# Self-attention with values as weights: two heads side by side in 64-column tiles

## The reference

```python
def causal_block_attention(q, k, v, scale, log_decay=None):
    ...
    def one_block(args):
        i, qi = args[0], args[1]
        s = jnp.einsum('bhqd,bhkd->bhqk', qi, k, preferred_element_type=jnp.float32) * scale
        if log_decay is not None:
            s = s + args[2][..., :, None] - log_decay.astype(jnp.float32)[:, :, None, :]
        ...
        s = jnp.where(mask, s, jnp.finfo(jnp.float32).min)
        p = jax.nn.softmax(s, axis=-1)
        return jnp.einsum('bhqk,bhkd->bhqd', p.astype(v.dtype), v)
```

## Time and profile before

| | us |
|---|---|
| runs, median of 3 | 3243.78 |
| profiled execution, its own time | 3245.3 |
| span of the profile | 3243.0 |
| self-attention stage, from the first scores to the last values | 392.5 to 755.5 |
| TensorE busy, whole span | 2861.4 (88%) |
| VectorE busy, whole span | 1193.4 (37%) |
| ScalarE busy, whole span | 612.3 (19%) |
| mean granted TensorE clock, share of full speed | 0.944 |

### The profile page before, as it was taken

One profiled execution on the slowest core, in us unless ns is written; L12 is line 12 of the kernel. 1 busy time (PEld: TensorE's weight loads), 2 busy tenths in 40 slices (PEclk: granted clock), 3 DMA queues, 4 the chain that ended last, 5 costly groups with the idle time before them and its releaser, 6 DMA issues.

```text
span 3243.0 us, 53552 instructions
## 1 busy us (share of the span) xinstructions
PE 2861.4 (88%) x19249; PEld 2455.6 (76%) x19250; DVE 1193.4 (37%) x3107; ACT 612.3 (19%) x1355; POOL 196.7 (6%) x257
## 2 busy tenths in 40 slices
PE   7999899999999996879988889899989998898980
PEld 5444477775477765879988889889989998898980
DVE  1111166663212226324322234323335443343446
ACT  0333233332011111111110111111111111111211
POOL 0000000001000001001000000000001000000100
PEclk9999899999999997989999999899999998999995
DMA  6111311122100006557554567456557875676737
GB/s 246 43 55 45 106 35 44 45 88 80 71 33 0 0 0 247 205 191 257 199 191 157 199 239 292 176 185 226 216 219 283 295 280 195 227 273 228 288 121 265
DMA packets 91043, 530.87 MB, mean 164 GB/s; under 512 B 20528, under 2 KB 42224, under 8 KB 65264
## 3 DMA queue, kind: packets, MB, share of 16 engines
q1 hardware_dynamic: 70992, 490.27, 41.8%
q0 software_dynamic: 18720, 33.60, 2.9%
q10 hardware_dynamic: 1152, 4.19, 0.3%
HBM read 510.14 MB, written 52.46 MB: 173 GB/s over the span
## 4 chain that ended last, share of the span: by engine, by line
PE 83%; issue 8%; DVE 4%; DMA 2%; ACT 2%; DVEq 1%; ACTq 1%; POOL 0%; POOLq 0%; SPq 0%
PE bank L989 48%; PE wide L989 22%; PE bank L982 5%; PE wide L1092 4%; PE bank L1109 3%; DMA ye<-d_y 1%; PE bank L1273 1%; DVE acc L1840 1%; ACT prob L819 1%; ACT st_q L799 1%; DVE mx L1497 1%; DVEq L1799 0%; PE wide L1095 0%; DVE biased L1502 0%; DVE act_t L1805 0%
## 5 line engine op out<-in xcount | busy, mean ns | idle before, releaser
L989 PE MATMUL bank<-xe_t,slot 128*128 128x128 f32 (+2 forms) x8192 | 1089.9, 296 | 187.2 <-issue 187.2
L989 PEld LDWEIGHTS bank<-xe_t,slot 128*128 128x128 f32 x8192 | 1077.2, 197 | 194.8 <-issue 194.3
L989 PE MATMUL wide<-act_t,slot 128*128 128x128 f32 (+2 forms) x4096 | 535.1, 290 | 8.4 <-DVE act_t L1805 7.6
L989 PEld LDWEIGHTS wide<-act_t,slot 128*128 128x128 f32 x4096 | 522.9, 191 | 13.3 <-DVE act_t L1805 13.2
L1793 DVE TENSOR_SCALAR glu<-bank,b_gu 128x256 f32<-128x256 f32 x256 | 123.8, 484 | 1011.3 <-PE bank L989 999.4
L931 ACT ACTIVATE sig<-glu 128x256 f32<-128x256 f32 x256 | 106.7, 417 | 1070.3 <-DVE glu L1793 1016.4
L989 PE MATMUL bank<-w_in,xt 128*128 128x512 f32 (+1 forms) x512 | 216.5, 579 | 3.8 <-DVEq L1426 3.8
L938 ACT ACTIVATE y_t<-wide,b_dn 128x256 f32<-128x256 f32 x256 | 107.3, 470 | 461.1 <-PE wide L989 461.1
L989 PEld LDWEIGHTS bank<-w_in,xt 128*128 128x128 f32 x512 | 96.7, 191 | 111.1 <-issue 110.4
L689 POOL DMA_INDIRECT xg<-d_xn,gidx x66 | 68.2, 1034 | 1727.8 <-DVEq L1708 1717.7
L1805 DVE TENSOR_TENSOR act_t<-lin,sig 128x256 f32<-128x256 f32 x256 | 109.3, 427 | 39.9 <-issue 5.0
(11 more groups left out here) (242 smaller groups left out, 2488.0 us busy)
## 6 DMA issues: line engine op xcount, KB each, us to landing
slot<-in_w_gu SPq DMA_DIRECT2D x128, 2048.0 KB, 7.8
slot<-in_w_dn SPq DMA_DIRECT2D x64, 2048.0 KB, 7.8
ye<-d_y SPq DMA_DIRECT2D x8, 2048.0 KB, 10.4
w_in<-in_w_in SPq DMA_DIRECT2D x1, 6144.0 KB, 30.9
w_mem_k<-in_w_mem_kv SPq DMA_DIRECT2D x1, 4096.0 KB, 15.8
w_mem_v<-in_w_mem_kv SPq DMA_DIRECT2D x1, 4096.0 KB, 25.6
x_sb<-in_x SPq DMA_DIRECT2D x8, 512.0 KB, 3.6
cneg<-d_cneg SPq DMA_DIRECT2D x8, 512.0 KB, 4.9
```

The lines of the kernel that those rows point to most:

```text
L989: m = pe.matmul(dst, l, r_, start=(k == 0), stop=(k == n - 1))
```

## The change

The steps of a pass are put in another order: each block row is now done for MLA head h and forget head h in turn, so `B_STEPS` runs (MLA 7, forget 7, MLA 0, forget 0, MLA 6, ...). In `values` the operands are swapped: 64 columns of values are held and 128 columns of transposed probabilities are streamed. The MLA head's product goes to PSUM partitions 0 to 63 and the forget head's to 64 to 127, in two column tiles of TensorE, block by block in turn. The result is transposed (values by queries), so VectorE copies it to SBUF (`turned`), TensorE transposes it back (`turn_back`), and `attended` scales both halves into `o_sb`. The values of a head are first copied by GpSimd from `v_mla` and `v_fox` into `v_head`. Transposed probabilities have four buffers, queries, keys and biases two of each (`side`), `biased` has one. The load of `w_xq` is moved behind the stage's barrier, among the loads of the next stage. Some semaphores are merged so that their number suffices.

```diff
-        B_STEPS = [(0, i) for i in long_short] + [(1, i) for i in long_short]
-        B_FIRST, B_LAST = (0, NT), (NT - 1, 2 * NT - 1)
+        B_STEPS = [(y, i) for i in long_short for y in range(2)]
+        B_FIRST, B_LAST = (0, 1), (2 * NT - 2, 2 * NT - 1)
@@ SyncE
-            load(w_xq[:, :, :], rows(a["w_xq"][0]), ld["w_xq"])
             barrier(sp, 3)
-            load(w_xo[:, :, :], rows(a["w_xo"][0]), ld["w_xo"])
-            load(w_r[:, :, :], rows(a["w_router"][0]), ld["w_r"])
-            with sp.Fori(0, NT) as i:
+            x_rows_again(0)
+            load(w_xq[:, :, :], rows(a["w_xq"][0]), ld["x_weights"])
+            x_rows_again(1)
+            load(w_xo[:, :, :], rows(a["w_xo"][0]), ld["x_weights"])
+            load(w_r[:, :, :], rows(a["w_router"][0]), ld["x_weights"])
+            with sp.Fori(2, NT) as i:
+                x_rows_again(i)
@@ GpSimd
+            def head_values(h, u, b):
+                po.wait_ge(b_v[b].free, u + 1)
+                for y, v in enumerate((v_mla, v_fox)):
+                    c = po.tensor_copy(v_head[b][y][:, :, :], v[:, :, bass.ds(h * S.DV, S.DV)])
+                c.then_inc(b_v[b].full, 1)
@@ TensorE
-                for j in range(i + 1):
-                    m = pe.matmul(pp[b][:, 0:S.DV], prob_t[b][:, j, :], v[:, j, bass.ds(h * S.DV, S.DV)],
-                                  start=j == 0, stop=j == i)
-                return m.then_inc(b_po[b].full, 1)
+                for j in range(i + 1):
+                    for y in range(2):
+                        m = pe.matmul(pp[b][y * S.DV:(y + 1) * S.DV, 0:P], v_head[side][y][:, j, :],
+                                      prob_t[b][y][:, j, :], start=j == 0, stop=j == i,
+                                      tile_position=(0, y * S.DV))
+                m.then_inc(b_po[b].full, 1)
+
+            def turn_back(h, k):
+                pe.wait_ge(b_turned, NT * h + k + 1)
+                pe.transpose(pp[k % 2][:, P:2 * P], o_turned[k % 2][:, :], ident).then_inc(b_out, 1)
...
-                    if n >= 1:
-                        values(h, n - 1)
-                values(h, 2 * NT - 1)
+                    if pair >= 1 and y == 0:
+                        values(u, side, pair - 1)
+                    if pair >= 1 and y == 1:
+                        turn_back(h, pair - 1)
+                values(u, side, NT - 1)
+                turn_back(h, NT - 1)
@@ VectorE
+            def turned(u, side, k):
+                b, h = k % 2, 2 * u + side
+                ve.wait_ge(b_po[b].full, b_po[b].base + NT // 2 * h + k // 2 + 1)
+                ve.tensor_copy(o_turned[b][:, :], pp[b][:, 0:P]).then_inc(b_turned, 1)
...
+            def attended(h, k):
+                i, b = B_STEPS[2 * k][1], k % 2
+                ve.wait_ge(b_out, NT * h + k + 1)
+                for y in range(2):
+                    m = ve.tensor_scalar(o_sb[:, i, bass.ds(h * S.DV + y * FW, S.DV)],
+                                         pp[b][:, P + y * S.DV:P + (y + 1) * S.DV], rr[:, 2 * k + y:2 * k + y + 1],
+                                         None, ALU.mult)
+                m.then_inc(b_po[b].free, 1)
```

More of the change, by code:

```diff
@@ L186, in build @@
         rr = r("rr", [P, 16])
-        r = Region(159, 175)
-        qt = [r("qt_mla", [S.DQ, T]), r("qt_fox", [S.DN, T])]
-        kt = [r("kt_mla", [S.DQ, T]), r("kt_fox", [S.DN, T])]
+        o_turned = [r(f"o_turned{b}", [P, P]) for b in range(2)]
         w_xq = Region(175, 207)("w_xq", [P, KD, D])
@@ L317, in b_groups, with b_ahead, b_heads @@
             return plan, used
-        def b_ahead(h, n, last):
+        def b_ahead(u, side, n, last):
             if n < 2 * NT:
-                return h, n
-            return None if last else (h + 1, n - 2 * NT)
-        def b_loop(eng, body):
-            with eng.Fori(0, H - 1) as h:
-                body(h, False)
-            body(H - 1, True)
+                return u, side, n
+            return None if last else (u + side, 1 - side, n - 2 * NT)
+        def b_heads(eng, body):
+            with eng.Fori(0, H // 2 - 1) as u:
+                for side in range(2):
+                    body(u, side, False)
+            body(H // 2 - 1, 0, False)
+            body(H // 2 - 1, 1, True)
         B_PLAN, B_PT = b_groups()
@@ L335, in build @@
         ld = {n: sem("ld_" + n) for n in (
-            "small", "mem", "w_mem_k", "w_mem_v", "w_in", "rope", "w_o", "w_xq", "w_xo",
-            "w_r", "bias", "g_fin")}
+            "small", "mem", "w_mem_k", "w_mem_v", "w_in", "rope", "w_o", "x_weights",
+            "bias")}
         stage_end, passed = sem("stage_end"), sem("passed")
@@ L357, in build @@
         c_pt = [b_pt[b].after(B_PT[b] * H) for b in range(2)]
-        c_pp = [b_po[b].after(NT * H) for b in range(2)]
+        c_pp = [b_po[b].after(NT // 2 * H) for b in range(2)]
         x_pt = [c_pt[b].after(NT) for b in range(2)]
@@ L380, in build @@
         a_st = [Handoff(sem, f"a_st{g}") for g in range(7)]
-        b_in = [Handoff(sem, f"b_in{y}") for y in range(2)]
-        b_cneg = Handoff(sem, "b_cneg")
+        b_in = [[Handoff(sem, f"b_in{side}{y}") for y in range(2)] for side in range(2)]
+        b_cneg = [Handoff(sem, f"b_cneg{side}") for side in range(2)]
         b_s = [Handoff(sem, f"b_s{b}") for b in range(2)]
@@ L387, in build @@
         b_ptd, b_pta = sem("b_ptd"), sem("b_pta")
+        b_v = [Handoff(sem, f"b_v{b}") for b in range(2)]
+        b_turned, b_out = sem("b_turned"), sem("b_out")
         c_ss, c_rstd, c_ot, c_h = sem("c_ss"), sem("c_rstd"), sem("c_ot"), sem("c_h")
@@ L641, in _ @@
             barrier(po, 2)
+            def head_values(h, u, b):
[3 more added lines that the diff above has]
+                c.then_inc(b_v[b].full, 1)
+            with po.Fori(0, H // 2) as u:
+                for b in range(2):
+                    head_values(2 * u + b, u, b)
             barrier(po, 3)
@@ L807, in _, with b_exp @@
             barrier(ac, 2)
[L810 removed]
+            for hd in (*b_in[0], *b_in[1], *b_cneg, *b_s, *b_p):
                 ac.sem_inc(hd.free, 1)
[L813 to L814 removed]
+            def b_exp(u, side, n):
+                (y, i), b, h = B_STEPS[n], n % 2, 2 * u + side
                 L = P * (i + 1)
@@ L1091, in scores @@
                     last = c + w == L
-                    m = pe.matmul(wide[b][:, c:c + w], ql, kt[y][:, c:c + w], start=True, stop=not last)
+                    m = pe.matmul(wide[b][:, c:c + w], ql, kt[side][y][:, c:c + w], start=True, stop=not last)
                     if c == 0 and after is not None:
@@ L1156, in _ @@
             barrier(pe, 4)
-            pe.wait_ge(ld["w_xq"], 16)
-            pe.wait_ge(ld["w_xo"], 16)
+            pe.wait_ge(ld["x_weights"], 48)
             def x_turn(i, kind):
@@ L1527, in b_body @@
                     ve.reciprocal(rr[:, n:n + 1], rs[:, n:n + 1])
-                    if nxt := b_ahead(h, n + 2, last):
+                    if nxt := b_ahead(u, side, n + 2, last):
                         row_max(*nxt)
                     ve.drain()
-                    if n >= 1:
-                        attended(h, n - 1)
-                attended(h, 2 * NT - 1)
-            row_max(0, 0)
-            row_max(0, 1)
-            b_loop(ve, b_body)
+                    if pair >= 1 and y == 0:
+                        turned(u, side, pair - 1)
+                    if pair >= 1 and y == 1:
+                        attended(h, pair - 1)
+                turned(u, side, NT - 1)
+                attended(h, NT - 1)
+            for hd in b_v:
+                ve.sem_inc(hd.free, 1)
+            row_max(0, 0, 0)
+            row_max(0, 0, 1)
+            b_heads(ve, b_body)
             barrier(ve, 3)
```

143 lines of the change are left out of this document (75 added, 68 removed).

## The result

The changed kernel takes 3285.96 us, median of 4 runs (3280.55 to 3287.21), against 3244.59 of the kernel before: a ratio of 1.0126, 95% interval 1.0108 to 1.0143. The prediction, 3236 and at most 3270, is wrong on the slower side. The profiled execution took 3285.54, its span is 3283.7.

The account below looks back on a forecast made before the run. TensorE bounds self-attention; work, form changes and waits sum to 43.1 us a pass against 44.4, about -10 over eight passes, +2 once: -8, 3237, in runs 3236. Its own range was 3226 to 3246, the whole 3215 to 3270.

Parts of the forecast that it names:

- The values product: Self-attention: two column tiles stream at once, 0.056 us a record, 8.1 a pass; upper bound 16.1.
- overlap by halves: Rival for the values product: loads cannot go ahead of waiting matmuls, 0.080 us a record, 3257 us; chance 0.15.
- tiles that don't overlap: Rival for the values product: streams stay one after another at 0.112 us, 3286 us; chance 0.18.
- The form of the array: TensorE going in and out of the column form around each values product: 0.3 us each, 2.4 a pass.
- No cost for the column form: Rival: the 0.3 us change of form may belong to row forms alone, 3223 us; chance 0.12.
- The work: TensorE's work in a self-attention pass without waits: 42.8 us before the change.
- The waits: TensorE's waits in a self-attention pass, from the new order of steps: 5.2 us against 1.6 before.
- The turning back: Last transposing back of a pass waits 1.95 us for VectorE's copy, with nothing to cover it.
- the clock: Rival: a gap of 2 us a pass halves TensorE's clock for some 3 behind it, +24, 3260; chance 0.05.
- Everything behind it shifted and not changed: Sign: stages behind self-attention only shift, by about 8 us shorter; wrong if one outside moves by more than 3.
- What costs nothing: GpSimd's value copies, second query and key buffers, w_xq load behind the barrier: free; uncovered loads would be 2 to 5 us.

Follow-up runs that it names:

- e3: Changed kernel with the values product's two loops exchanged, all MLA blocks in their column tile, then all forget blocks in theirs: 3315.04 us, ratio 1.0229.
- e2: Changed kernel with each transpose bank given to one copying engine, first four blocks to VectorE's, the rest to ScalarE's: 3259.32 us, ratio 1.0066.
- e5: Changed kernel with the values product and turning back one step later, and each transpose bank given to one copying engine: 3233.97 us, ratio 0.9972.
- e6: Changed kernel with the values product and turning back one step later, old alternation of transpose banks kept: 3243.23 us, ratio 1.0002.
- e8: Changed kernel with VectorE's eight self-attention passes written out instead of a loop over two at a time: 3272.38 us, ratio 1.0095.
- e9: e5 with VectorE's eight self-attention passes written out as well: 3219.36 us, ratio 0.9926 to the kernel before.
- e7: Kernel before with 500 TensorE transposes that never run, in a branch not taken ahead of the expert loop: 3256.74 us, ratio 1.0045.
- e1: Changed kernel with 50 useless TensorE transposes a pass put where TensorE waits: 3267.01 us, ratio 1.0077.
- e4: Changed kernel's order, buffers, banks and loops, but the values product of before, without column tiles or turning back: 3324.26 us, ratio 1.0265.

## Why the prediction was wrong, step by step

- **The values product, right.** V at 0.056 a record, forecast 8.1 a pass; measured 0.055. Taking the lower bound was right, and e3 shows what the upper was: 0.110 with the tiles not in turns. The rival "overlap by halves" (0.080), which rested on the Trainium skill ("TensorE: Matmul & The Clock Gate", Part 3), finds no support: both tiles have all rows, and the records are 0.055 apart. The measured 3286 is also the figure that the prediction gave for tiles that don't overlap, but by chance: the pitch of 0.112 that this rival needs is not there.
- **The form of the array, right.** 0.23 measured against 0.3; "No cost for the column form" is out. The rule of the Trainium skill ("TensorEngine Tiling (Array Packing)", Key Properties) that a change of the tiling mode drains the engine agrees with these 0.23.
- **The work, right.** 42.8 for the kernel before (43.5 by the window), 37.9 for the changed one without the waits; with the slow clock taken off, the changed kernel, e2, e5, e6, e8 and e9 give 38.3 to 39.0.
- **The waits, right in sum and wrong in kind.** "Waits: 5.2 a pass against 1.6 before"; measured 5.8 against 0.9. The turning back was foreseen (1.57 of 1.95). But the walk priced latency from scores to transposes and VectorE's turn, and left out the bank: 23.6 of the 36.4 us of waits from 437 to 755 are for ScalarE's copy. It also left out VectorE's ways back. That the sum came out near is luck: the other 3.3 of the 5.2 were priced as latency, and where they were expected 3.6 a pass for the bank was measured (e2, without that, still waits 2.1 a pass there for VectorE's copies).
- **The step that failed: the clock.** The sum takes all work of the stage at full clock, and the waits at their own length only. The loss by the clock stood among the rivals, with a chance of 0.05: "A gap of 2 a pass could do the same to some 3 behind it: +24". It was the case that came true, and larger: 4.9 a pass, 39 over eight. Added to the forecast's 43.1 that is 48.0, of the 49.1 measured. The argument against it, that the stretches near 1220 were sparse on both sides, was read from one place and did not hold: in e5 one wait of 2.71 is followed by 14 us at half clock without a gap. No row of the kernel before settles it. Its stage has a low clock only at the start (0.50 from 392 to 400), behind 12 us in which TensorE was busy for 2.8.
- **"Everything behind it shifted and not changed": right up to the experts (30.9 and 30.6), wrong for them.** 10.3 of the 41 are there; e7 shows that a longer program of TensorE ahead of that loop alone can do as much. That it did so in this kernel was not tried by itself (the other engines' programs grew too), so the cause of these 10 stays open.
- **What costs nothing, right.** Values copied by GpSimd, second buffers, w_xq behind the barrier: the first tile's last sum behind the stage came 30.7 later, and the stage's end 30.9.

What stays open is how deep the clock falls for given waits. e1 waits 3.0 a pass and has 0.98; e4 waits 2.9 and has 0.84; e8 waits 5.2 and has 0.95. That waits bring the clock down is shown from two sides, by filling them (e1) and by removing them (e2, e5, e9). But no sum of waits predicts the clock. A part of the reason is to be seen in e4: in a slow stretch TensorE is the late one and hardly waits, so the stretch that the waits set off counts none itself. What ends such a stretch no run here shows.

## What to carry to other kernels

Once a saving leaves an engine with idle time, ask what the clock does with it: here 5.8 us of short waits in 49 cost another 4.9, all that the work had shrunk by (42.8 to 37.9). Another bank, one product a step later and one loop written out turned +31 us in the stage into -35, with the same arithmetic. When an order changes, walk each engine's queue for every shared buffer, not only for latency: the bank that two neighbours now share stands behind the other engine's longest instruction. And compare the idle time in the loops that were not touched, because longer code ahead of them can move the time by 10 us or more, up or down.

## What the runs showed of the hardware that was not expected

- Two column tiles of fp32 stream side by side, although each product is two records of one tile in a row: 0.055 us a record of 128 columns in turns, 0.110 one tile after the other.
- At the way back of VectorE's loop over two passes it idles 2.6 to 2.8 us; over one pass, in the kernel before, none of its idle times without a releaser is longer than 0.4 between 437 and 755, and written out it is gone.
- After short waits TensorE's granted clock stays at 0.50 for much longer than they last, under full load: 14 us behind one wait of 2.71 (e5), 24 us behind two of 1.00 and 1.38 (e4).
- 500 instructions that never run, ahead of a loop with large branches, cost 14.7 us; 200 gained 12 in one kernel and nothing in the other.
